# Hybrid decoder step: the eighth weight part of the expert ring is asked for right behind the seventh

## The reference

```python
x = x + merge_heads(pool_mixer(u), stick_breaking(q, k, v), w_out)   # [u|q|k|v] = rms_norm(x) @ w_in
h = rms_norm(x, norm_ffn)
g = argmax(softmax(h @ w_group))               # one of 4 groups
top_v, top_i = top_k((h @ w_expert)[g], 2)     # 2 of its 8 experts
gate = p_group[g] * softmax(top_v)
x = x + sum(gate_j * (silu(h @ w_gate[e_j]) * (h @ w_up[e_j])) @ w_down[e_j])
```

## Time and profile before

| what | value |
|---|---|
| three runs: median, lowest, highest | 1122.19, 1121.57, 1123.5 us |
| span of the profiled execution | 1122.4 us |
| PE busy | 1092.5 us, 97% |
| DVE, ACT, POOL busy | 443.6, 332.1, 171.0 us |
| the queue of SP's DMAs | 273.69 MB, 64.9% of 16 engines' span |
| expert stage, from the first gate and up matmul | 564.0 us to the end |

### The profile page before, as it was taken

One profiled execution on the slowest core, in us unless ns is written; L12 is line 12 of the kernel. 1 busy time (PEld: TensorE's weight loads), 2 busy tenths in 40 slices (PEclk: granted clock), 3 DMA queues, 4 the chain that ended last, 5 costly groups with the idle time before them and its releaser, 6 DMA issues.

```text
span 1122.4 us, 26874 instructions
## 1 busy us (share of the span) xinstructions
PE 1092.5 (97%) x11636; PEld 796.1 (71%) x11636; DVE 443.6 (40%) x816; ACT 332.1 (30%) x649; POOL 171.0 (15%) x150
## 2 busy tenths in 40 slices
PE   8999999999999999999899999999999999999995
PEld 7999999966665559999766666666666666666663
DVE  5326653378875443345722212212212222122121
ACT  6423332166775552223211111111111111111111
POOL 0001200699100000000001111111111111111110
PEclk9999999999999999999899999999999999999998
DMA  7356684000126459464699999999999999999991
GB/s 253 105 158 215 197 272 137 1 13 2 39 78 187 130 207 293 151 261 182 253 343 401 381 392 389 391 381 386 392 369 394 387 388 386 390 394 388 388 341 30
DMA packets 85694, 293.04 MB, mean 261 GB/s; under 512 B 13375, under 2 KB 44799, under 8 KB 59957
## 3 DMA queue, kind: packets, MB, share of 16 engines
q1 hardware_dynamic: 78405, 273.69, 64.9%
q0 software_dynamic: 7168, 17.58, 6.6%
HBM read 272.98 MB, written 42.87 MB: 281 GB/s over the span
## 4 chain that ended last, share of the span: by engine, by line
PE 90%; DVE 4%; DMA 3%; ACT 1%; issue 1%; POOL 0%; SPq 0%; ACTq 0%; POOLq 0%; DVEq 0%
PE bank L2099 13%; PE bank L2521 11%; PE bank L2525 10%; PE bank L2529 9%; PE bank L2331 8%; PE bank L2555 5%; PE bank L2559 5%; PE bank L2563 4%; PE bank L2142 4%; PE bank L2308 3%; PE bank L2271 3%; PE bank L2500 2%; PE bank L2180 2%; DMA wo_raw<-in_w_out 2%; PE bank L2541 1%
## 5 line engine op out<-in xcount | busy, mean ns | idle before, releaser
L2521 PE MATMUL bank<-w_ring,xeT 128*32 128x256 f32 x1536 | 342.6, 380 | 0.0
L2525 PE MATMUL bank<-w_ring,xeT 128*32 128x512 f32 x1536 | 265.8, 594 | 0.7 <-ACT xeT L1509 0.7
L2521 PEld LDWEIGHTS bank<-w_ring,xeT 128*32 128x32 f32 x1536 | 166.6, 110 | 54.1
L2555 PE MATMUL bank<-w_ring,hT 128*32 128x256 f32 x768 | 171.7, 380 | 0.0
L2529 PE MATMUL bank<-w_ring,xeT 128*32 128x256 f32 x1536 | 155.9, 379 | 0.0
L1970 DVE SCALAR_TENSOR_TENSOR hid<-sgl,gtab,bank 96x256 f32<-96x256 f32 x32 | 21.9, 683 | 337.6 <-ACT sgl L1515 337.6
L2559 PE MATMUL bank<-w_ring,hT 128*32 128x512 f32 x768 | 133.2, 595 | 1.6 <-ACT hT L1521 1.6
L2099 PE MATMUL bank<-w_hi,xh 128*128 128x256 f32 (+1 forms) x424 | 121.9, 287 | 0.0
L2099 PE MATMUL bank<-w_lo,xh 128*128 128x256 f32 (+1 forms) x424 | 119.1, 281 | 0.0
L2099 PE MATMUL bank<-w_hi,xl 128*128 128x256 f32 (+1 forms) x424 | 119.0, 281 | 0.0
L1708 DVE TENSOR_TENSOR_SCAN keep<-keep,unseen 128x1024 f32<-128x1024 f32 (+7 forms) x64 | 94.6, 1510 | 38.0 <-ACT keep L1293 37.9
(11 more groups left out here) (282 smaller groups left out, 1648.3 us busy)
## 6 DMA issues: line engine op xcount, KB each, us to landing
w_ring<-in_w_gate SPq DMA_DIRECT2D x64, 1024.0 KB, 29.3
w_ring<-in_w_up SPq DMA_DIRECT2D x64, 1024.0 KB, 26.5
w_ring<-in_w_down SPq DMA_DIRECT2D x64, 1024.0 KB, 29.4
k_scr<-in_cache_k SPq DMA_DIRECT2D x32, 256.0 KB, 3.4
v_scr<-in_cache_v SPq DMA_DIRECT2D x32, 256.0 KB, 3.5
pgk<-k_scr SPq DMA_DIRECT2D x32, 256.0 KB, 4.0
w_raw<-in_w_in SPq DMA_DIRECT2D x7, 1024.0 KB, 6.3
pgv<-v_scr SPq DMA_DIRECT2D x4, 1024.0 KB, 6.7
```

What stands on the lines that cost most here:

```text
L2521: return pe.matmul(up_right_ps(i, g), xeT[i][:, k, rows_of(g)], w[1][:, k, FA:F], start=first and g != 1, stop=ends, skip_group_check=True)
L2525: pe.matmul(gate_ps(i)[rows_of(g), :], xeT[i][:, k, rows_of(g)], w[0][:, k, :], start=first, stop=ends, skip_group_check=True)
L2555: return pe.matmul(y_right_ps(g), hT[:, ft, rows_of(g)], w[:, ft, DA:D], start=first and g != 1, stop=ends, skip_group_check=True)
```

## The change

Part 7 is asked for right behind part 6, after the last output product and ahead of the last tile's stores; it was asked for with part 8, after the first two gathers had landed. Part 8 stays where it was.

```diff
@@ -972,6 +972,7 @@
                 if t == LAST:
                     sp.wait_ge(s_wo, len(wsteps))
                     load_part(6)
+                    load_part(7)
                 if t == 7:
                     sp.wait_ge(s_wo, tile_done(t))
                     load_part(4)
@@ -990,8 +991,7 @@
 
             for i in range(2):
                 sp.wait_ge(s_gl[i], 16)
-            for q in (7, 8):
-                load_part(q)
+            load_part(8)
             sp.wait_ge(s_yst, 16 * NT)
             sp.wait_ge(s_lgp, NT)
             load_part(9)
```

## The result

The changed kernel takes 1129.55 us (1128.25 to 1130.32) against 1122.47: the ratio is 1.0047, with a 95% interval of 1.0034 to 1.0060. The two medians stand further apart, 7.1 us or 1.0063; the record does not show why the ratio is lower. Two further measurements of the same kernel, each beside the kernel before, gave 1.0057 (1.0044 to 1.0070) and 1.0060 (1.0047 to 1.0073). So the change costs 5 to 7 us; I had forecast 1.6, and a range up to 1127.0. The first span is 1126.5 us against 1122.4.

The account below looks back on a forecast made before the run. PE (TensorE), 90% of the chain, was taken to bound the kernel. Nothing gained from earlier weights and 1.6 us lost to the later first gather gave 1123.8 us against 1122.19, with a range of 1121.9 to 1127.0.

Parts of the forecast that it names:

- Weights earlier are worth nothing: Expert stage: PE waits for no DMA, so moving part 7 earlier gains nothing there.
- The stores behind part 7: Last tile's stores in SyncE's queue: 5.1 us more ahead of them, y_all landing at 559.5 (559.3 to 560.0).
- The exchange of waits: POOL before its first gather: the wait for DVE's table gives way to a longer one for the stores.
- How much longer: POOL before its first gather: y_all lands 2.1 us after the table, where it had landed 3.0 us before it.
- From landing to gather: From y_all's landing to POOL's first gather: 0.82 us, so the gather starts at 560.3, 1.9 us later.
- The scatter that I took as the nearest row: Scatter of 595.05, landing at 604.35 with the next gather 0.82 us later; the model for a landing releasing a gather.
- the 1.04 behind the table: Kernel before: the first gather started 1.04 us after DVE's table was ready; the forecast took 0.82 instead.
- The 0.3 of slack: Between the first gather's landing, 562.19, and PE's transposes, 562.52: absorbs 0.3 us, leaving PE 1.6 us later.
- Rival B: PE between fillers and first expert: the granted clock falls again, 2.5 us more, 1126.3 (1123.8 to 1128.9); chance 0.22.
- the 1.56 of 1105.4: From 1105.4 to 1107.0 PE was busy 0.04 of 1.60 us and the clock stayed at 1.00.
- the way out that the prediction took from it: SyncE's queue: completion is not first-in first-out, so the stores might pass part 7 and the sum would be 0.

Follow-up runs that it names:

- second and third executions: The changed kernel, unedited, run and profiled again twice: 1129.89 us, ratio 1.0057, and 1130.41 us, ratio 1.0060, to the kernel before.
- the third of the kernel before: The kernel before, unedited, run and profiled a third time: ratio 0.9994 to the kernel before, span 1123.2 us.

## Why the prediction was wrong

*Weights earlier are worth nothing: right.* PE meets no wait for `w_ring` in any execution, and from the first L2541 to the end all six of the two kernels take the same within 0.4 us.

*The stores behind part 7: right, in part by luck.* 10.3 us from issue to landing was forecast, 10.3, 10.9 and 10.7 were measured. The sum went by a queue that is full up to the landing. The queues from 558 to 560 us (packets, MB, share of the time of 16 engines), first execution, then second:

```profile
q1 hardware_dynamic: 44, 0.16, 19.1%
```
```profile
q1 hardware_dynamic: 164, 0.60, 75.7%
q8 instruction: 1, 0.02, 3.0%
```

19.1% of 16 engines are three, while y_all landed only at 560.6. In the second and third executions the DMA share is under 0.1 from 560.0 and from 559.5 on, and the landings came at 561.7 and 561.3. So each landing came 1.7 us and more after most engines were through. Why a few of them trail is not shown; an instruction fetch like that of the q8 row was in flight in all three (in the first from 556 to 558), so it does not tell them apart. The first execution also differs in its queue: its part 5 was issued 4.9 us ahead of part 6, against 2.8 in the trace that the sum was made from, and 3.1 and 3.4 in the other two. So less stood ahead of its stores, and a few engines took longer; that the two come out at 10.3 exactly is luck.

*The exchange of waits: right.* "The wait for the table gives way to a longer one" is what happened.

*How much longer: wrong, the first failed term.* I set the landing 2.1 us behind the table by taking the table's time from the one execution that I had, 557.39. There the clock fell at 552.1, just ahead of PE's last work for the table. In the other five executions of the two kernels it fell later or not in that work, and the table was ready 12.5 to 12.9 us after part 6's issue, instead of 13.9. So the landing is 3.2 to 3.9 us behind the table.

*From landing to gather: 1.09 us, not 0.82.* It was 1.08 to 1.09 in the three executions, and with half a part and with two parts ahead. The scatter that I took as the nearest row was not the nearest kind; the 1.04 behind the table was. The first gather moved from 14.2 to 17.5 us after part 6's issue on average, by 3.2 instead of 1.9; to the first transposes 2.8 are left, where I had 1.6. The 0.3 of slack that I took off is 0.4 to 0.5: from the start of the gather to the transposes it is 4.1 to 4.2 us in before, 3.7 where PE waits for it.

*Rival B was the case, and I gave it 0.22.* The clock fell a second time in all three executions. I had judged the gap in PE as 1.5 us of idleness, and set it beside the 1.56 of 1105.4 that left the clock alone. That length rested on fillers that end 19.1 us after part 6's issue, again taken from the one execution; here they end after 18.3, 18.2 and 15.4 us (in the third they ran at full clock), and PE's wait is 2.5, 3.3 and 5.9 us. Its price, 2.5 as I put it, was about right: 1.4, 2.8 and 2.8.

With these terms the sum is 2.8 + 2.3 = 5.1 us. The three ratios give 5.3, 6.4 and 6.7, the medians of the first 7.1. Of what is left, 0.7 lies ahead of part 6 in the profiled executions, where the dips near 509 and 532 are and where the third of the kernel before has one as well; that this part is chance is likely but not shown, and without it up to 1.6 us of the third ratio, 2.0 of the first medians, stay open.

The Trainium skill, page "DMA: Bandwidth & Descriptors", section "Queues, rings and completion order", has as its case of a later transfer that completes first one on a single DMA engine behind one on 16, and says that an engine's completion signal lands only after that engine's earlier writes. That is narrower than the way out that the prediction took from it. No execution here shows the stores ahead of part 7: they landed 10.3 to 10.9 us after their issue.

## What to carry to other kernels

An empty stretch of the DMA queue is no offer if a transfer that somebody waits for is issued into the same queue before the new one is through: sum the queue up to the next awaited landing, and set it against what the waiter waits for otherwise, not against the engines' idle time. Where the consumer is bound by TensorE and its loads never make it wait, asking for them earlier has no upside, and any place ahead of a store that gates the next stage is a risk. Take a slack that decides a sum from several executions, and look what the clock did in each of them: a us of slack in one profile was a us of half clock.

## What I had not expected of the hardware

- A second hardware queue does not put a small transfer first. 0.19 MB issued by ACT beside two parts in SyncE's queue took 7.0 us to land, against 10.3 to 10.9 behind the same two parts in one queue, and 3.6 to 5.9 us in SyncE's queue with part 6 alone ahead (six executions). From 552 to 556 us ACT's queue moved 0.39 MB, both stores, and SyncE's 1.27 MB beside it.
- The length of PE's idleness alone does not say whether the granted clock falls: it held over a wait of 2.7 us (half of part 7 ahead) and of 2.3 us (more fillers in the changed kernel), and fell after one of 1.8 us (fillers ahead of the rank matmuls alone) and of 2.5 us (the changed kernel).
- A gather of 96 rows that starts with the DMA engines free holds PE's first transposes back for 3.6 to 3.7 us, and for 4.85 with the end of 2 MB still in flight.
